# Weight tiles of a decoder step, loaded in two halves of 64 partitions

## The reference

```
layer 0:  y = s5_mixer(rmsnorm(x)) ; x = x + y
          x = x + swiglu(rmsnorm(x), w_ffn_gate_up, w_ffn_down)        # dense, 2816 wide
shared:   kv = rmsnorm(x) @ w_kv
layer 1:  q = rmsnorm(x) @ w_q ; x = x + sink_attention(q, k, v) @ w_o
          x = x + moe_swiglu(rmsnorm(x), w_router, w_exp_gate_up, w_exp_down)
out:      rmsnorm(x), the states, the last 128 keys and values

def moe_swiglu(h, ...):      # top 2 of 8 experts, each 3584 wide
    for e in range(8):
        out = out + comb[..., e:e + 1] * swiglu(h, w_gu[e], w_down[e])
```

## Time and profile before

| | us |
|---|---|
| runs | 1739.66, 1742.06, 1744.48 |
| median | 1742.06 |
| profiled execution | 1742.76 |
| its span | 1741.0 |
| PE busy | 1629.3 (94%) |
| DVE busy | 1280.0 (74%) |
| ACT busy | 936.7 (54%) |
| mean granted clock of TensorE | 0.926 |

### The profile page before, as it was taken

How to read it: one execution, slowest core, us unless ns; L and a number is a source line. 1 busy time by engine, 2 the same in 40 slices (tenths; PEclk the granted TensorE clock), 3 DMA queues, 4 the chain that set the end, 5 groups by cost and what they waited for, 6 DMA issues and landing times.

```text
span 1741.0 us, 20428 instructions
## 1 busy us (share of the span) xinstructions
PE 1629.3 (94%) x8458; PEld 1366.7 (79%) x8459; DVE 1280.0 (74%) x1207; ACT 936.7 (54%) x817; POOL 98.7 (6%) x123
## 2 busy tenths in 40 slices
PE   5979878999988988899999999999999999999995
PEld 2469778999977767788888888888888888888884
DVE  7967345565355435688988988998988988898884
ACT  2022034333335423576776777776676776776772
POOL 2660010200010000000000000000000000000000
PEclk8986689999999558899999999999999999999997
DMA  1000055955545002499998999998999998999990
GB/s 64 13 12 1 7 218 182 237 214 175 180 159 199 21 1 97 172 359 366 350 366 309 348 363 365 351 357 316 347 360 366 347 362 315 346 361 362 353 353 27
DMA packets 61651, 422.26 MB, mean 243 GB/s; under 512 B 8142, under 2 KB 8294, under 8 KB 11505
## 3 DMA queue, kind: packets, MB, share of 16 engines
q1 hardware_dynamic: 58496, 411.03, 62.2%
q0 software_dynamic: 3056, 9.85, 2.9%
HBM read 413.97 MB, written 6.88 MB: 242 GB/s over the span
## 4 chain that ended last, share of the span: by engine, by line
PE 91%; DVE 5%; ACT 2%; issue 1%; DMA 1%; SPq 0%; DVEq 0%; ACTq 0%
PE ps L1388 24%; PE ps L1389 24%; PE ps L1390 23%; PE ps L1295 3%; PE ps L1366 2%; PE ps L1367 2%; PE ps L1576 1%; PE ps L1598 1%; PE ps L1277 1%; PE ps L1380 1%; DVE WL L973 1%; PE ps L1316 1%; PE ps L1341 1%; PE ps L1471 1%; PE ps L1498 1%
## 5 line engine op out<-in xcount | busy, mean ns | idle before, releaser
L973 DVE TENSOR_TENSOR WL<-raw,WH 128x2048 fp32r<-128x2048 f32 x387 | 885.3, 2291 | 214.5 <-ACT WH L516 206.1
L516 ACT CAST WH<-raw 128x2048 fp32r<-128x2048 f32 x387 | 738.7, 1910 | 206.2 <-PE ps L1390 202.2
L1388 PE MATMUL ps<-WH,XEH 128*128 128x512 f32 x896 | 360.4, 402 | 2.4 <-issue 2.4
L1389 PE MATMUL ps<-WL,XEH 128*128 128x512 f32 x896 | 354.9, 396 | 0.0
L1390 PE MATMUL ps<-WH,XEL 128*128 128x512 f32 x896 | 354.4, 395 | 0.0
L1390 PEld LDWEIGHTS ps<-WH,XEL 128*128 128x128 f32 x896 | 168.2, 188 | 42.8
L1388 PEld LDWEIGHTS ps<-WH,XEH 128*128 128x128 f32 x896 | 169.1, 189 | 40.7 <-issue 2.6
L1389 PEld LDWEIGHTS ps<-WL,XEH 128*128 128x128 f32 x896 | 169.0, 189 | 36.6
L1388 PE MATMUL ps<-WH,AFH 128*128 128x512 f32 x448 | 179.1, 400 | 1.6 <-DVE WL L973 1.6
L1390 PE MATMUL ps<-WH,AFL 128*128 128x512 f32 x448 | 177.6, 396 | 0.0
L1389 PE MATMUL ps<-WL,AFH 128*128 128x512 f32 x448 | 177.5, 396 | 0.0
(11 more groups left out here) (356 smaller groups left out, 1944.4 us busy)
## 6 DMA issues: line engine op xcount, KB each, us to landing
raw<-in_we SPq DMA_DIRECT2D x336, 1024.0 KB, 5.1
raw<-in_wd SPq DMA_DIRECT2D x51, 1024.0 KB, 4.9
bias_rows<-SC POOLq DMA_DIRECT2D x1, 3072.0 KB, 36.2
BIAS<-bias_rows POOLq DMA_DIRECT2D x16, 128.0 KB, 9.0
X<-in_xT SPq DMA_DIRECT2D x1, 1056.0 KB, 5.0
out_yT<-XN SPq DMA_DIRECT2D x2, 528.0 KB, 2.7
out_ks<-KCT POOLq DMA_DIRECT2D x1, 1024.0 KB, 8.0
out_vs<-VC POOLq DMA_DIRECT2D x1, 1024.0 KB, 9.9
```

The lines of the kernel that those rows point to most:

```text
L516: a.copy(WH[tile[2] % SPLIT][:, :], raw[slot_][:, :]).then_inc(sem("hi_made"), 1)
L973: v.tensor_tensor(WL[tile[2] % SPLIT][:, :], raw[tile[2] % RING][:, :], hi_, ALU.subtract)\
L1388: t_.matmul(out, sh, mh, start=first, stop=False)
L1389: t_.matmul(out, sh, ml, start=False, stop=False)
```

## The change

Each load of a weight tile becomes two, one for partitions 0 to 63 and one for 64 to 127, issued by SP one behind the other. The wait for a free buffer stands once, ahead of the first. Both count the same semaphore, so ACT's wait goes from 16 to 32 for each filling of a buffer.

```
         def loads(eng, tile):
             r, stride, c = tile
-            value = 16 * (c // RING + 1)
-            return value if r is None else eng.snap(r * (16 * stride // RING) + value)
+            value = 32 * (c // RING + 1)
+            return value if r is None else eng.snap(r * (32 * stride // RING) + value)
...
             for n in range(RING):
-                sp.dma_start(raw[n][:, :], wd[n]).then_inc(loaded[n], 16)
+                for half in range(2):
+                    rows = slice(64 * half, 64 * half + 64)
+                    sp.dma_start(raw[n][rows, :], wd[n][rows, :]).then_inc(loaded[n], 16)

             def load(tile, src):
                 free = at(sp, tile, 1 - RING)
                 sp.wait_ge(split, free)
-                sp.dma_start(raw[tile[2] % RING][:, :], src).then_inc(loaded[tile[2] % RING], 16)
+                for half in range(2):
+                    rows = slice(64 * half, 64 * half + 64)
+                    sp.dma_start(raw[tile[2] % RING][rows, :], src[rows, :]).then_inc(loaded[tile[2] % RING], 16)
```

## The result

The changed kernel takes 2100.64 us (median; 2085.85 to 2109.64) against 1742.13 us: 1.205 times the time before, with a 95% interval of 1.198 to 1.212. The prediction was 2184 us in a range of 1900 to 2450. The profiled execution took 2085.85 us for a span of 2084.1.

The account below looks back on a forecast made before the run. PE bounds the expert layer before, its loads after the change: 327 x 4.36 = 1425.7 us plus 754.8 us for the rest, 1.9 us at the first tile and 1.8 us around the span give 2184 us, range 1900 to 2450.

Parts of the forecast that it names:

- The bound of before: Expert layer: PE sets the pace at 2.99 us per tile, loads hidden at 2.49 us, 17% of slack.
- The second issue: SP's extra issue per tile, 0.65 us for two in a 2.99 us period: cost 0.
- All 16 engines on each half, one half behind the other: Each 64-row load goes over all 16 engines, four rows on each; both halves stand in the same 16 queues.
- Half the rate at worst: Expert loads into 64 partitions: at worst 210 GB/s, 4.98 us per tile.
- The row of bias_rows: Store reading 16 SBUF partitions: 98 GB/s at a share of 0.98 against 421, read as a narrow SBUF side.
- The middle, 4.36 us per tile: Expert loads: engines partly share, between 3.74 us at random points and 4.98 us in step; partial sharing's chance 0.53.
- the power law through 16 and 128 partitions: Rate of expert loads into 64 partitions: 0.615 of full, 259 GB/s, 4.05 us per tile.
- The first tile and the dense layer: Ahead of the expert layer: first dense tile's data time rises by 1.9 us; other dense loads stay hidden, 0.
- All engines in step: Rival, expert layer: all engines fill the same half together, 4.98 us per tile, 2387 us; chance 0.28, including a little beyond.
- Free halves: Rival, expert layer: halves cost nothing, PE stays the bound, 1743 us; chance 0.11.
- The clock: Rival, expert layer: PE's granted clock falls to 0.50, 5.6 us per tile, 2590 us; chance 0.05, shared with over 5.17 us.
- What would show it: Expert layer: waits at nearly every tile, share above 0.9 at 210 to 280 GB/s, landings over 15 us; dense span unchanged.

Follow-up runs that it names:

- runs of 8 packets: Against the changed kernel, every second tile loads its upper half first, so each engine has 8 packets in a row for one side: 2213, 2218, 2229, 2265 us.

## Why the prediction held, and which term was off

**The bound of before.** Right: 17% of slack in the loads decided it. Every kernel whose expert loads kept up with PE stayed within 0.3% of before.

**The second issue, at nothing.** Right: halves by columns and by even and odd rows cost some 0.1%.

**All 16 engines on each half, one half behind the other.** Right as far as it shows: the queue closes each half with sixteen packets, the share is 1.02 at 260 GB/s, and the queue's order counts.

**Half the rate at worst.** Right: 216 GB/s from 720 to 800 us in the changed kernel, 4.85 us per tile, against the 4.98 that the sum of two equal halves allowed. The row of bias_rows, 16 partitions at a quarter of the rate, pointed the right way.

**The middle, 4.36 us per tile.** This is the term that was mis-sized. Measured: (2032.2 - 719.2) / 326 = 4.03 us. 327 x 0.33 = 108 us too much, against 98 us between the forecast span of 2182.4 and 2084.1; the other terms of the sum came out within some 10 us together (the first issue at 719.2 instead of 717.6 us, for one). What failed in it is the picture of the overlap: I had let two partners stand at random points of their halves from the start. They start in step and drift, the rate moves between 216 and 336 GB/s, and 4.03 is the mean over a course that the prediction didn't have. That this mean lies near a middle taken between two ends is in part luck, and so is the power law through 16 and 128 partitions, which gave 4.05.

**The first tile and the dense layer.** Right: 1.5 to 2 us at the first tile, nothing behind it.

**The rivals.** All engines in step is what the expert layer began with, and with runs of 8 packets the rate stayed near there until 1600 us (207 to 223 GB/s); it didn't last in the change. Free halves: excluded by the changed kernel, and shown to exist where each transfer reaches all parts of the 128. The clock: it fell a little (0.98 over the layer; down to 0.86 in a stretch of the run with 8 packets), and the chain of work ran through the loads, so it didn't set the time.

**What would show it.** The signs came nearly as given: ACT's wait for landings, 310 times for 333 tiles (PE's for a split, 221 times, is less than "at nearly every tile"), a landing of 17.7 us, a share above 0.9 at a low rate, a dense layer of the same length. The rate's upper sign, 280 GB/s, was passed in the middle of the layer.

## What to carry to other kernels

Before a load is cut in pieces, ask which partitions the pieces fill at the same moment, not how many there are: cut by columns or by alternate rows, the 1 MiB tile kept up with PE as the whole one did, at 351 GB/s; cut into lower and upper partitions, at half to four fifths of the rate with every engine busy. Read the slack first, as the bytes of a tile over the rate of a stretch with a full queue against the time in which the tile is used: 2.49 against 2.99 us here, so a loss of 17% is free and the next per cent is not. And a high DMA share beside a low rate, as in the store of 16 partitions, was the sign here that something behind the engines is narrow.

## What the runs showed of the hardware

A transfer confined to partitions 0 to 63 or 64 to 127 keeps 16 engines busy at 216 GB/s, in a stream of such halves that starts in step; its row packets take 0.628 us where they took 0.309 in whole tiles. The stream then speeds up to 336 GB/s over some 850 us while the engines drift apart (a tile's landing signals 3.0 us from first to last, then 10.7). Why it falls back is open.

An issue of a 64-row load took SP at least 0.465 us, one of 128 rows 0.327 us (also at half the columns). Copies of 8 contiguous rows of 8 KiB between two places of HBM went out as 16 packets of 4 KiB each; with the rows cut to 8128 bytes, as 8 packets.
